# The expert dot products of a PEER layer: VectorE multiplies, ScalarE sums

## The reference, cut to what matters

```python
eidx = jnp.take_along_axis(cand_i, pos, axis=-1)         # (token, head, 16)
g = jax.nn.softmax(top_s, axis=-1)
u = expert_down[eidx]
a = jax.nn.gelu(jnp.einsum('thkd,td->thk', u, xb), approximate=False)
coef = (g * a.astype(jnp.float32)).astype(xb.dtype)
return jnp.einsum('thk,thkd->td', coef, expert_up[eidx])
```

## Time and profile before

| | |
|---|---|
| median of 3 runs | 1374.96 us (1373.96 to 1375.88) |
| the profiled execution | 1376.12 us, of which the span from first to last instruction is 1374.4 us |
| busy in the span | TensorE 1250.8 us, VectorE 929.7, ScalarE 648.4, GpSimd 291.4 |
| gathers | 36864 packets, 268.45 MB on the software queue |
| stage of the experts | from the first gather (223.3 us) to the end of the last products (881.1 us) |

### The profile page before, as it was taken

The page is one execution under the profiler, slowest core; times in us unless marked ns, Lnnn a source line. Parts: engine busy times, 40 slices in busy tenths (PEclk is TensorE's granted clock), DMA queues, the critical chain, the costliest instruction groups (busy, mean ns, idle before and its releaser), DMA issues.

```text
span 1374.4 us, 15434 instructions
## 1 busy us (share of the span) xinstructions
PE 1250.8 (91%) x5496; PEld 861.5 (63%) x5496; DVE 929.7 (68%) x1836; ACT 648.4 (47%) x1302; POOL 291.4 (21%) x281
## 2 busy tenths in 40 slices
PE   8999999988887878878787778899999999999998
PEld 8887898543343434334343234488788888888887
DVE  5767667976777776676766676655766556877445
ACT  5657554434333343433333344565556744655334
POOL 1000002544444344344444454000000000000000
PEclk9999999999999999999999999999999999999999
DMA  7543539999999999999999999745354445555551
GB/s 291 196 170 120 182 111 376 395 421 421 421 421 422 421 421 421 421 422 421 408 422 422 421 415 421 294 168 173 120 190 174 154 155 183 182 184 187 201 193 62
DMA packets 57268, 398.74 MB, mean 290 GB/s; under 512 B 7128, under 2 KB 7640, under 8 KB 9448
## 3 DMA queue, kind: packets, MB, share of 16 engines
q0 software_dynamic: 36864, 268.45, 47.2%
q1 hardware_dynamic: 18288, 126.10, 25.7%
q10 hardware_dynamic: 2040, 3.19, 0.7%
HBM read 396.67 MB, written 1.05 MB: 289 GB/s over the span
## 4 chain that ended last, share of the span: by engine, by line
PE 61%; DMA 26%; DVE 5%; ACT 4%; issue 2%; POOL 1%; SPq 0%; ACTq 0%; DVEq 0%
PE ps L861 37%; DMA B<-in_ex,eidx 25%; PE ps L1246 11%; PE ps L889 4%; DVE B L2621 3%; PE ps L890 2%; POOL B L825 1%; ACT diags L1814 1%; DVE hl L2117 1%; ACT av_ L1806 1%; PE ps L1141 1%; ACT hl L1533 1%; DMA ring<-in_wt 1%; PE ps L1124 1%; PE ps L1106 1%
## 5 line engine op out<-in xcount | busy, mean ns | idle before, releaser
L1246 PE MATMUL ps<-B,diags 128*128 128x512 f32 x1024 | 482.5, 616 | 112.3 <-ACT diags L1814 112.1
L1246 PEld LDWEIGHTS ps<-B,diags 128*128 128x128 f32 x1024 | 188.7, 194 | 376.7 <-issue 194.4
L2621 DVE CUSTOM_DVE_ANT_0 B<-B 128x1024 f32<-128x1024 f32 x256 | 311.7, 1223 | 163.1 <-DMA B<-in_ex,eidx 160.2
L825 POOL DMA_INDIRECT B<-in_ex,eidx x256 | 285.3, 1115 | 570.2 <-PE ps L1246 330.2
L2117 DVE TENSOR_TENSOR hl<-ring,hl 128x2048 fp32r<-128x2048 f32 x110 | 251.7, 2291 | 168.9 <-ACT hl L1533 168.7
L1533 ACT ACTIVATE hl<-ring 128x2048 fp32r<-128x2048 f32 x110 | 210.1, 1912 | 128.1 <-PE ps L861 125.3
L861 PE MATMUL ps<-hl,R 128*128 128x512 f32 x900 | 209.2, 391 | 0.3 <-DVE R L2133 0.3
L861 PE MATMUL ps<-hl,XT 128*128 128x512 f32 (+1 forms) x888 | 205.6, 390 | 3.0 <-DVE hl L2117 2.5
L1801 ACT ACTIVATE av_<-av_ 128x2 f32<-128x2 f32 x128 | 26.0, 203 | 369.3 <-DVE av_ L2621 369.3
L861 PEld LDWEIGHTS ps<-hl,R 128*128 128x128 f32 x900 | 167.7, 188 | 35.6 <-DVE R L2133 0.7
L861 PEld LDWEIGHTS ps<-hl,XT 128*128 128x128 f32 x888 | 163.6, 189 | 39.0 <-DVE hl L2117 4.0
(11 more groups left out here) (393 smaller groups left out, 1023.2 us busy)
## 6 DMA issues: line engine op xcount, KB each, us to landing
ring<-in_wt SPq DMA_DIRECT2D x112, 1024.0 KB, 4.8
raw<-in_wt SPq DMA_DIRECT2D x4, 1024.0 KB, 7.6
B<-in_ex,eidx POOLq DMA_INDIRECT x256, 12.7
X<-in_x SPq DMA_DIRECT2D x2, 512.0 KB, 5.0
B<-in_mem ACTq DMA_DIRECT2D x1, 1024.0 KB, 9.3
PW<-in_wple SPq DMA_DIRECT2D x1, 1024.0 KB, 8.0
ring<-in_wt SPq DMA_DIRECT2D x2, 512.0 KB, 4.1
out<-B SPq DMA_DIRECT2D x3, 256.0 KB, 2.0
```

What stands on the lines that cost most here:

```text
L825: e.indirect_dma_start(out=rows[i % NG][:, :], out_offset=None, in_=A["ex"], in_offset=bass.IndirectOffsetOnAxis(ap=eidx[:, tb, s:s + 1], ...
L1246: m = e.matmul(acc[tb][hf][:, :], diags[:, i % 4, :], rows[i % NG][:, 1024 + 512 * hf:1536 + 512 * hf], start=(s == 0), stop=(s == 127))
L2621: m = e.tensor_tensor_reduce(R[:, 0:1024], R[:, 0:1024], XG[:, tb, :], 1.0, 0.0, ALU.mult, ALU.add, av_[:, tb, s + z:s + z + 1])
```

## The change

VectorE's fused instruction becomes a plain product of the same operands, which still overwrites the down row. The sum goes to ScalarE: ahead of the GELU of a pair, two copies, each of one product row onto itself, with the running sum written into the column of `av_`, and a wait for them.

```diff
             def row_gelu(i, tb, s):
                 e.wait_ge(*dot[i // 2])
+                for z in range(2):
+                    R = rows[(i + z) % NG]
+                    d = step(e.activation(R[:, 0:1024], R[:, 0:1024], ACT.Copy, accum_out=av_[:, tb, s + z:s + z + 1]))
+                e.wait_ge(*d)
                 d = step(e.activation(av_[:, tb, s:s + 2], av_[:, tb, s:s + 2], ACT.Gelu))
...
                         for z in range(2):
                             R = rows[(i + z) % NG]
                             e.wait_ge(*gath[i + z])
-                            m = e.tensor_tensor_reduce(R[:, 0:1024], R[:, 0:1024], XG[:, tb, :], 1.0, 0.0, ALU.mult,
-                                                       ALU.add, av_[:, tb, s + z:s + z + 1])
+                            m = e.tensor_tensor(R[:, 0:1024], R[:, 0:1024], XG[:, tb, :], ALU.mult)
                         m.then_inc(dot.sem)
```

## The result

The changed kernel took 1395.98 us in the median of 4 runs (1394.76 to 1397.78), the kernel before 1374.46 us beside it (4 runs, 1373.30 to 1375.88): 1.0158 times as long, with a 95% interval of 1.0143 to 1.0173. So it is slower by 21.5 us, where 10.5 us had been forecast; the direction and the range held, the size did not. The two profiled executions lie closer together than the medians (1394.76 us, the fastest of the four, and 1376.12 us, above all four of the kernel before), 18.6 us apart.

The account below looks back on a forecast made before the run. The chain of waits put the stage's bound on a loop paced by gathers at 420 GB/s, not on one engine. Terms 4.4 + 1.7 + 4.4 = 10.5 us on 1374.96 gave 1385.5 us; 8-in-10 range 1377 to 1400.

Parts of the forecast that it names:

- Operations and path: Every pair: two ScalarE copies add 2.2 us between dot and GELU; VectorE's plain product saves nothing; ScalarE stays below full.
- Start, +4.4: Stage start: copies ahead of the first GELU and behind `scores_block(1)` send gather 10 and later ones out 4.4 us later.
- a bound of 2.9 us: Stage start: possible extra 2.9 us if TensorE, idle longer, does the second pair at its lower clock, 1.2 GHz.
- my 7.0: Shortest gather wait in the trace, 7.0 us at gather 10, taken as a wait without any queue.
- the 1.8 us of loss: Stage start: loss if a gather alone takes 4.4 us, leaving 2.6 us of queue as cover; sum then 7.9 us.
- First table change, +1.7: Behind the fifth pair: ScalarE's 1.7 us lateness has no cover while the gather queue is short; bounds 0 to 3.0.
- Steady part, 0: Steady loop: longer buffer holds and lateness at table changes cost nothing, covered by the queue of gathers.
- Rival B: Steady loop loses pace, three places a window at 1.5 us each: 32 us on top, 1417 us; chance 0.16.
- its part of 5 to 10 us: Partial steady-loop loss of 5 to 10 us, held as likely as the whole loss under Rival B.
- End, +4.4: Stage end: copies of pair 125 delay `final_turned`, those of pair 126 follow; last 16 products start 4.4 us later.
- Rival A: Copies covered at the start and at `final_turned`; only the last pair's 2.2 us remain, 1377.2 us; chance 0.09.

Follow-up runs that it names:

- a step for each row: Changed kernel with VectorE raising its semaphore after each row, so the first copy runs beside VectorE's second product; 1388.12 us, ratio 1.0087.
- fillers: Changed kernel plus 16 constant products of 128 columns on TensorE behind the third pair of most half-rounds, copies left as they are; 1388.42 us, ratio 1.0102.
- the three places: Changed kernel with the fused product kept for pairs 0 and 1, the pair behind each table change and the last three pairs; together 1379.33 us, ratio 1.0039.

## Why the prediction was right and where it was wrong

**Operations and path: right.** A copy 1047 ns (1045 taken), 2.20 us a pair (2.2 taken), VectorE's product unchanged, ScalarE 62 to 65 of 79.5 us busy (66 to 69 forecast), median wait for a gather 10.4 us (10.6 forecast).

**Start, +4.4: right in size, in part by luck.** Row 16 shows +3.9. Gather 10 goes out 4.0 us later, 4.5 counted from the stage's begin. But the two changes of clock at the first two pairs, 1.3 us back and 1.7 us lost, nearly cancel; the sum had them at nothing (the second as a bound of 2.9 us). Keeping the fused product in two pairs takes 3.5 us away at row 24. The estimate from the Trainium skill ("DMA: Bandwidth & Descriptors", section "Anatomy of one DMA"), 4.4 us for a gather by itself, fits the 5.5 us seen now better than my 7.0 did; but the 1.8 us of loss that followed from it is not what rows 12 to 16 show (+2.7 to +3.4). Gather 10 wasn't without a queue, and its delay reached the later rows all the same. As a term in a sum it was worth less: undone alone it brings 2.2 us, since the ring behind takes a part of it.

**First table change, +1.7: wrong place.** There rows 16 to 24 lose 0.3 us: the cover that the prediction missed is the work that TensorE had in arrears. But between rows 24 and 32 3.3 us arise. The prediction had `scores(1)` nowhere: it followed who waits for ScalarE on TensorE's side and not VectorE, which in this place waits for a result that follows pair 7 through TensorE and ScalarE. The run with `scores(1)` moved shows that it isn't the order on ScalarE, the run with a step for each row that a shorter path removes it. What share VectorE's wait and the slow pair behind it have stays open: waits of 3.48, 4.51 and 6.81 us (a step for each row; changed; fused at the start) go with 3.70, 5.34 and 6.53 us for the pair and losses of 0.5, 3.3 and 4.3 us.

**Steady part, 0: this is the step that failed**, "I charge the steady pairs nothing; the cover is the queue of gathers". The working gave the gathers behind a table change 8.9 us. In the trace they have 6.4 to 8.9. It left out two things: the GELU's table load moved onto the path (it was counted as ScalarE's lateness, 1.7 us, not as TensorE's idle time), and TensorE at half speed, mostly behind a gap of 2.75 to 3.6 us, takes 1.4 to 3.0 us longer for the next products. In place of nothing, 4.9 us were lost from row 32 to row 255. The bound of 2.9 us for just that stood in the start's step, and not here. Rival B named the sign (traffic under 415 GB/s) and the places; its size, 1.5 us at each of three places in every window, was far too high; the 4.9 us lie just under its part of 5 to 10 us; and its reason, that full traffic needs gathers 10.4 us ahead, is contradicted: with the pair behind each change fused, waits of 9 to 10 us go with 421 GB/s, and with fillers 8 us do.

**End, +4.4: right.** 5.1 us, through `final_turned`; 3.4 come back with the last three pairs fused, and nearly all where the other places are fused too. It is one execution's figure: in the other runs that keep the last pairs' full copies, without a step for each row, 12.2 to 14.8 us pass there; the changed kernel has 12.5.

**The rest**: 1.6 us arise after the stage, which the prediction didn't have and which come and go without regard to the change (below); 2.9 us are the difference between the medians and the profiled pair. That the time stayed in the range is owed to its upper end, which had been set for rival B's partial cases. Rival A, and with it the rule of the Trainium skill that it leaned on ("Perfetto Trace Analysis", section "Identifying the Most-Contended Engine": look to the engine with the highest occupancy), falls: ScalarE, at 47% before and 66% after, was never that engine, and 1.6% were lost through it.

## What to carry to other kernels

Work moved to an idle engine is free only where it isn't on a ring: list every place where an engine waits for something that follows the lengthened step, on all engines, the one that gave the work away included. Price a gap on TensorE at the products behind it too, since they may run at half speed, and ask whether the queue of transfers, shortened by the same change, still covers that. And where two table sets alternate, look at which instruction the load now stands in front of: a cheap copy ahead of the GELU put 1.28 us on the path that had been hidden.

## What was not expected of the hardware

Losses did not add up: the three places undone one by one give 2.2, 1.9 and 5.2 us, which make 9.3; undone together they give 16.7.

A gap on TensorE doesn't always cost clock. In the changed kernel the same gap of 3.47 us was followed by no slow product (584 us) and by seven (502 us). Ahead of the first pair the same gap of 1.78 us was followed by 6.57 us of products in the kernel before and by 3.67 with the fused product kept there. So a single execution of one place can't price it; the count over 15 places can.

From the last expert products to the end of the span, 14 profiled kernels took 493.2 us (six), 494.9 (six) or 496.5 (two), in steps of 1.6 us, without regard to the change. In that part TensorE is busy throughout at a granted clock of 1.00 and does 115 to 116 products in 20 us instead of 117 where the longer time is seen. Why stays open; differences of 2 us between single executions of this kernel mean little.
